# Up units of the gated networks: 64-column products in pairs instead of 128-column products

## The chip, the cores and the metric

The kernel runs on one core of a Trainium2 chip. The metric is the device time of one execution in microseconds. A core has a matrix engine (PE, which the profile splits into its matmuls, PE, and its weight loads, PEld), a vector engine (DVE), an activation engine (ACT), a general engine (POOL), and 16 DMA engines that the queues of SP, ACT and POOL feed.

## What is computed

Two stacks of two layers each, on 256 tokens of 1,024 values in float32. The first stack has two kinds of attention, a gated network of width 2,816 in its first layer (a "dense" network) and eight experts of width 3,584, of which each token takes two, in its second. Each layer of the second stack has a gated network, a mixer with three branches, and another gated network. The part that matters here is the gated network, of which there are five in all (one dense, four in the second stack):

```
def swiglu(h, w_in, w_out):
    a, b = jnp.split(h @ w_in, 2, axis=-1)      # 1024 -> 2 x 2816
    return (jax.nn.silu(a) * b) @ w_out         # 2816 -> 1024
```

## The kernel before

All weights are streamed once through a ring in the on-chip memory. The ring has four slots of 6,144 words in each partition (SLOTS, UNIT), and a slot's first 4,096 words take one 2 MB load. SP issues the loads in order (lines 434 and around), each as soon as PE has counted the slot's last use in the semaphore unit_used.

A network (the function network, line 647) has eleven up units of 256 columns of each of the two weight matrices (FFN_STEPS), and then the down products. The first up unit (whole_unit) is made as plain products of 128 columns of weights over all 1,024 rows, and in the networks of the second stack in two token halves of 128. The other ten (up_unit, line 672) are made by a scheme that needs seven block products where a plain 2 x 2 block product needs eight: DVE adds and subtracts weight blocks ahead of time (sum_weights, four additions of 128x1024 per unit, lines 1585 to 1593) and token blocks once per network (sum_tokens), PE makes seven groups of products, and ACT and DVE fold the seven results into four (line 1304, and the seven additions of fold at lines 1616 to 1625).

Each of the seven groups is done for both weight matrices (m), and adds up four products (k, over half of the 1,024 rows), so an up unit has 7 x 2 x 4 = 56 products. Each has 128 rows and 128 columns of weights, 128 columns of tokens, and a result of 128x128 in PSUM. In float32 the trace shows every matmul call as two weight loads and two matmuls, called records below, so the unit has 112 records. The calls go through the helper product (line 597), which most of the kernel uses, so the records of the up units stand at L597 beside others.

```python
for j, (lhs, rhs) in enumerate(...):            # the seven groups, line 693
    for m in range(2):
        mm = product([(up_group(q, j, m), lhs(m, k), rhs(k)) for k in range(KT // 2)])
mm.then_inc(unit_used, 1)
```

An up unit waits first for its load, for its four sums of weights, and for the fold of the unit two before it (lines 675 to 679). Units 1 to 8 are two rounds of a hardware loop whose body holds four units (Fori, line 703); units 9 and 10 are straight code (line 706). up_group puts the results of a unit in four banks of PSUM, and the next unit's in the other four. ACT and DVE work on one unit's results while PE makes the next.

The down products follow (line 718): seven products of 128x128 weights by 512 columns for each of eleven pairs of hidden blocks, by the same scheme.

The experts already use calls of 64 columns in pairs: gather (line 763), chosen_up (line 788) and chosen_down (line 798) split 128 columns of weights in GROUPS = 2 strips of STRIP = 64 that write PSUM partitions 0 to 63 and 64 to 127, one after the other for each k. The moving side there has 96 columns of tokens for the three busiest experts and 80 for the other five (TIERS). Their loop body holds seven units of 32 + 16 calls and runs four rounds per expert.

Of the kernel before, what the change touches and what calls it, by code (L numbers as in the profile page):

```python
# [19 lines left out]
KT = D // P  # L20
# [67 lines left out]
GROUPS = 2  # L88
STRIP = P // GROUPS
# [106 lines left out]
def build(nc, a, out):  # L196

    with ExitStack() as ctx:
# [182 lines left out]
        def landed(c, turns):  # L381

            return loaded[c % SLOTS], 16 * (c // SLOTS + 1) + 16 * turns

        def up_weights(c):

            return slot(c, 2 * KT, FF_STEP).rearrange("p (m k) n -> p m k n", m=2)
# [6 lines left out]
        def up_group(u, j, m):  # L394

            at = j * SEQ + m * P
            return psum[:, 4 * (1 - u % 2) + at // 512, at % 512:at % 512 + P]
# [20 lines left out]
        def banks(jobs, name):  # L418
            b = 2 * FIXED_PAIR.get(name, jobs[name] % 4)
            return psum[:, b:b + 2]  # L420
# [160 lines left out]
        def _(pe):  # L581
# [4 lines left out]
            def count_unit(m):  # L586
                if open_units[0]:
                    m.then_inc(unit_used, open_units[0])
                    open_units[0] = 0
# [4 lines left out]
            def product(terms):  # L594

                for i, (o, lhs, rhs) in enumerate(terms):
                    m = pe.matmul(o, lhs, rhs, start=i == 0, stop=i == len(terms) - 1)  # L597
                    if i == 0 and len(terms) > 1:
                        count_unit(m)
                return m  # L600
# [46 lines left out]
            def network(which, c0, turns, begin=None, finish=None):  # L647
# [24 lines left out]
                def up_unit(u, q, t):  # L672

                    w, sums = up_weights(c0 + q), weight_sum[q % 2]
                    pe.wait_ge(*landed(c0 + q, t))
                    pe.wait_ge(*ffn["weight_sum"].by(which, 4 * u))
                    if q == 2:
                        pe.wait_ge(*ffn["gated"].by(which, 2))
                    pe.wait_ge(*ffn["folded"].by(which, FOLDS_AHEAD + 7 * (u - 2)))

                    def of_weights(i, kk):
                        return lambda m, k: w[:, m, kk * KT // 2 + k, i * P:(i + 1) * P]

                    def of_sums(j):
                        return lambda m, k: sums[:, j, m, k, :]

                    def of_tokens(kk, h):
                        return lambda k: xT[:, kk * KT // 2 + k, h * P:(h + 1) * P]

                    def of_token_sums(j):  # L690
                        return lambda k: token_sum[:, j, k, :]

                    for j, (lhs, rhs) in enumerate(((of_weights(0, 0), of_tokens(0, 0)), (of_sums(1), of_token_sums(1)),
                                                    (of_weights(0, 1), of_tokens(1, 0)), (of_sums(2), of_token_sums(2)),
                                                    (of_sums(0), of_token_sums(0)), (of_sums(3), of_tokens(1, 1)),
                                                    (of_weights(1, 1), of_token_sums(3)))):
                        for m in range(2):
                            mm = product([(up_group(q, j, m), lhs(m, k), rhs(k)) for k in range(KT // 2)])
                    mm.then_inc(unit_used, 1)

                whole_unit()
# [18 lines left out]
                for p in range(FFN_STEPS - 4):  # L720
                    pe.wait_ge(*landed(c0 + FFN_STEPS + p // 2, turns))
                    pe.wait_ge(*ffn["down_sum"].by(which, 8 * p + 8))
                    for name in ("P1", "P6", "P2", "P7", "P5", "P3", "P4"):
                        if p == 0 and name == "P5":
                            pe.wait_ge(*ffn["folded"].by(which, FOLDS_AHEAD + 7 * (FFN_STEPS - 1)))
                        m = down(p, name)
# [6 lines left out]
                for p in range(last - 3, last + 1):  # L733
                    pe.wait_ge(*landed(c0 + FFN_STEPS + p // 2, turns))
                    pe.wait_ge(*ffn["down_sum"].by(which, 8 * p + 8))
                    for name in ("P1", "P6", "P5", "P2", "P3"):
                        m = down(p, name)
# [7 lines left out]
                for name in ("P7", "P4"):  # L745
                    for p in range(last - 2, last + 1):
                        if name == "P4" and p == last and finish is not None:
                            finish()
                        m = down(p, name)
# [118 lines left out]
            for l in range(LAYERS):  # L868
# [8 lines left out]
                if l == 0:  # L877
                    for i in range(KT // 2):
# [3 lines left out]
                        for h in range(HALVES):  # L882
                            for k in (2 * i, 2 * i + 1):
                                m = pe.matmul(banks(J, "latent0")[:, h, :], xT[:, k, h * P:(h + 1) * P], w[:, k, :],  # L884
                                              start=k == 0, stop=k == KT - 1, skip_group_check=True)
                else:
                    pe.wait_ge(*landed(c, 0))
                    for h in range(HALVES):
                        pe.wait_ge(*f["turned_x"].by(0, 3 + h))
                        for k in range(KT):  # L890
                            if h == 0 and k == KT - 2:
                                turn_end(1)
                            m = pe.matmul(banks(J, "latent0")[:, h, :], xT[:, k, h * P:(h + 1) * P], w[:, k, :], start=k == 0, stop=k == KT - 1)
# [9 lines left out]
                for name in ("dq0", "dq1", "dk0", "dk1", "dv0", "dv1"):  # L903
# [7 lines left out]
                    if l == 0 and name in ("dq0", "dq1", "dk0", "dk1"):  # L911
# [3 lines left out]
                        for r in (2 * i, 2 * i + 1):  # L915
                            pe.wait_ge(*once["ind"].by(0, 2 + 8 * (r + 1)))
                            for n in range(4):
                                m = pe.matmul(banks(J, f"bias{i}")[32 * n:32 * n + 32, r % 2, 0:MAP], block_delta, reached[r % 2][:, n], start=True, stop=True)
# [8 lines left out]
                for name, k_tiles, width, source in (("uq", 3, 384, cqT), ("ukv", 2, 512, ckvT)):  # L927
                    pe.wait_ge(*landed(c, 0))
                    w = slot(c, k_tiles, 2 * width)
                    for h in range(HALVES):  # L930
                        pe.wait_ge(*banks_free(f"{name}{h}", l))
                        pe.wait_ge(*f["cqT" if name == "uq" else "ckvT"].by(l))
                        for n in range(2):
                            m = row_product(banks(J, f"{name}{h}")[:, n, 0:width], w, k_tiles, width, source, h, n * width)
# [3 lines left out]
                for name, source, ready in (("q", qrow, "q_rot"), ("k", kcat, "kcat")):  # L938
                    if name == "k":
                        pe.wait_ge(*f["kv_rows"].by(l))  # L940
                    for i in range(2):
# [3 lines left out]
                        for n in range(4):  # L945
                            for h in range(HALVES):
                                m = pe.transpose(o[0:MLA_QK, n * SEQ + h * P:n * SEQ + (h + 1) * P], source[:, h, 4 * i + n, :], ident[:])
# [9 lines left out]
                for i in range(MAPS1 + 3):  # L957
# [10 lines left out]
                    if i < MAPS1:  # L968
                        pe.wait_ge(*banks_free(f"scores{i}", l))
                        for m in range(2):  # L970
                            if i < PAIRS1:
                                q, k = qT[0:MLA_QK, 2 * i + m, :], kT[0:MLA_QK, 2 * i + m, :]
                            else:
                                q, k = dqT[64 * m:64 * m + 64, i - PAIRS1, :], dkT[64 * m:64 * m + 64, i - PAIRS1, :]
                            mm = map_scores(banks(J, f"scores{i}")[:, m], q, k)
                        mm.then_inc(f["full"].sem, 1)
                    if 0 <= i - 2 < MAPS1:
# [3 lines left out]
                        for m in range(2 if h < PAIRS1 else 1):  # L981
                            mm = turn_map(banks(J, f"turn{h}")[:, m], T[:, h % 2, m])
                        mm.then_inc(f["full"].sem, 1)
                    if 0 <= i - 3 < MAPS1:
# [4 lines left out]
                        if h < PAIRS1:  # L989
                            mm = pair_values(o, PT[:, h % 2], lambda m, half: vrow[:, half, 2 * h + m, :])  # L990
                        else:
                            w, vh = PT[:, h % 2, 0], dv[:, :, (h - PAIRS1) * P:(h - PAIRS1 + 1) * P]
                            pe.matmul(o[:, 0:P], w[:, 0:P], vh[:, 0], start=True, stop=True)
                            mm = product([(o[:, P:2 * P], w[:, P:2 * P], vh[:, 0]), (o[:, P:2 * P], w[:, 2 * P:MAP], vh[:, 1])])
# [35 lines left out]
                for h in range(HALVES):  # L1030
                    pe.wait_ge(*banks_free(f"mix{h}", l))
                    m = half_rows(J, f"mix{h}", m1T, h, c, 0, f["mT"].by(l, 3), f["mT"].by(l), (lambda: turn_x(0)) if h else None)
# [35 lines left out]
                for h in range(HALVES):  # L1068
# [4 lines left out]
                    m = half_rows(J, f"ple_gate{h}", xT, h, c, 0, ready, ready, rank_tokens if l == h == 1 else None, 0)  # L1073
# [28 lines left out]
            for l in range(LAYERS):  # L1102
# [42 lines left out]
                for h in range(HALVES):  # L1145
                    half_ready(1, h)
                    for k in range(KT):
                        if h == 0 and k == 5:
                            turn_half("mix", 1, 1)
                        m = pe.matmul(banks(J, "a_v")[:, h, :], xT[:, k, h * P:(h + 1) * P], w[:, k, :], start=k == 0, stop=k == KT - 1)  # L1150
# [13 lines left out]
                for h in range(HALVES):  # L1164
                    m = row_product(banks(J, "b_kv")[:, 1, h * P:(h + 1) * P], w, KT, P, xT, h, P)
# [14 lines left out]
                for g in range(A_GROUPS):  # L1180
                    for h in range(HALVES):
                        m = pe.matmul(o[:, g * SEQ + h * P:g * SEQ + (h + 1) * P], v2[:, h, g * P:(g + 1) * P], wsT[:, g, :], start=True, stop=True)
# [6 lines left out]
                for h in range(C_HEADS):  # L1189
                    m = pe.transpose(o[:, h * P:(h + 1) * P], c_kT[:, h, 0:P], ident[:])  # L1190
# [8 lines left out]
                for i in range(MAPS2 + 3):  # L1199
# [4 lines left out]
                    if i < MAPS2:  # L1204
                        pe.wait_ge(*banks_free(f"scores{i}", l))
                        for m in range(2):
                            mm = map_scores(banks(J, f"scores{i}")[:, m], bqT[64 * m:64 * m + 64, i, :], bkT[64 * m:64 * m + 64, i // 2, :])
                        mm.then_inc(s["full"].sem, 1)
                    if 0 <= i - 2 < MAPS2:
# [3 lines left out]
                        for m in range(2):  # L1213
                            mm = turn_map(banks(J, f"turn{h}")[:, m], T[:, h % 2, m])
# [10 lines left out]
                for h in range(C_HEADS):  # L1225
                    for n in range(HALVES):
                        m = pe.matmul(o[:, h * SEQ + n * P:h * SEQ + (n + 1) * P], c_kT[:, h, n * P:(n + 1) * P], c_qT[:, h, n * P:(n + 1) * P], start=True, stop=True)
# [7 lines left out]
                for h in range(C_HEADS):  # L1235
                    m = pe.matmul(o[:, h * C_V:(h + 1) * C_V], c_kw[:, h, :], cv[:, 0, h * C_V:(h + 1) * C_V], start=True, stop=True)
                m.then_inc(s["full"].sem, 1)
                for n in range(HALVES):
# [6 lines left out]
                    for h in range(C_HEADS):  # L1245
# [3 lines left out]
                        m = product(terms)  # L1249
# [21 lines left out]
                for h in range(HALVES):  # L1271
                    pe.wait_ge(*(s["ycT"] if h else s["gate"]).by(l))
                    m = half_rows(J, f"out{h}", m2T, h, unit[0], turns, s["mT"].by(l, 5), s["mT"].by(l), (lambda: turn_half("ffn2", 2, 0)) if h else None)
# [1095 lines left out]
```

## Time and profile before

| what | us |
|---|---|
| median of three runs | 3244.98 (3243.61 to 3247.26) |
| the profiled execution | 3246.58 |
| its span, first to last instruction | 3245.0 |
| PE busy in it | 3193.5 (98%) |
| PEld busy | 2624.8 (81%) |
| DVE busy | 1049.6 (32%) |
| ACT busy | 414.4 (13%) |

The page has the busy time of every engine, the span in 40 slices with the clock that PE was granted, the DMA queues, the chain of work that ended last (followed back from the last instruction), and the costliest groups of instructions. A busy time of PE sums overlapping records, whose latency is longer than the distance between two starts. So what a product costs is read from the length of an unbroken run of records divided by their number, as the chain in order of time gives both, and not from the mean length of a record.

### The profile page before, as it was taken

The numbers are of one execution on the slowest core, as the hardware profiler recorded it, in microseconds if no ns is written. First come the engines' busy times: TensorE is split into PE (matmuls) and PEld (weight loads), VectorE is DVE, ScalarE is ACT, GpSimd is POOL, SyncE is SP. The second block draws the span as 40 slices with busy tenths as digits, with TensorE's granted clock in tenths as the row PEclk, the third lists the DMA queues.
The fourth block names the chain that finished last, engine by engine and source line by source line (L and its number), as shares of the span: only waits on it lengthen the run. The fifth ranks groups of instructions, "written<-read, shape, count | busy, mean of one in ns | idle before, by whom it ended". The sixth has DMA issues, their size and how long they took to land.

```text
span 3245.0 us, 76028 instructions
## 1 busy us (share of the span) xinstructions
PE 3193.5 (98%) x34760; PEld 2624.8 (81%) x34760; DVE 1049.6 (32%) x2232; ACT 414.4 (13%) x1031; POOL 50.6 (2%) x86
## 2 busy tenths in 40 slices
PE   9999999999999999999998999999999999999999
PEld 6685985777699999999997966588895976688894
DVE  2252564043201101111013561211566562210465
ACT  1240000042111100000001001110100001110100
POOL 0000000000000000000000000000000000000000
PEclk9999999999999999999998999999999999999999
DMA  7423444333699899999996444334444444434442
GB/s 253 151 99 152 182 160 177 139 108 120 248 388 357 355 399 376 426 426 426 426 426 271 158 172 170 130 130 156 156 158 166 175 156 169 157 108 151 156 175 91
DMA packets 63087, 714.03 MB, mean 220 GB/s; under 512 B 7569, under 2 KB 9233, under 8 KB 11889
## 3 DMA queue, kind: packets, MB, share of 16 engines
q1 hardware_dynamic: 59328, 703.62, 55.7%
q0 software_dynamic: 1008, 5.94, 0.5%
q10 hardware_dynamic: 2624, 2.65, 0.4%
q8 instruction: 96, 1.57, 0.2%
q14 instruction: 31, 0.25, 0.0%
HBM read 709.30 MB, written 1.05 MB: 219 GB/s over the span
## 4 chain that ended last, share of the span: by engine, by line
PE 94%; DMA 3%; DVE 2%; ACT 1%; POOL 1%; issue 0%; SPq 0%; POOLq 0%; DVEq 0%; ACTq 0%
PE psum L597 50%; PE psum L788 15%; PE psum L718 10%; PE psum L798 8%; PE psum L853 5%; DMA weight_ring<-in_experts 3%; PE psum L817 1%; PE psum L1150 1%; PE psum L763 1%; PE psum L635 1%; PE psum L631 1%; PE psum L884 1%; POOL statistics L519 0%; PE psum L630 0%; PE psum L1124 0%
## 5 line engine op out<-in xcount | busy, mean ns | idle before, releaser
L597 PE MATMUL psum<-arena,weight_ring 128*128 128x256 f32 (+1 forms) x5408 | 974.2, 339 | 7.9 <-DVE arena L2069 3.8
L597 PEld LDWEIGHTS psum<-arena,weight_ring 128*128 128x128 f32 x5408 | 869.4, 191 | 98.4 <-issue 14.5
L788 PE MATMUL psum<-arena,weight_ring 128*64 128x80 f32 (+1 forms) x14336 | 570.5, 238 | 6.8 <-DMA weight_ring<-in_experts 2.6
L788 PEld LDWEIGHTS psum<-arena,weight_ring 128*64 128x64 f32 x14336 | 547.9, 137 | 16.1 <-issue 8.1
L597 PE MATMUL psum<-weight_ring,arena 128*128 128x128 f32 (+3 forms) x3024 | 511.2, 326 | 2.0 <-DVE arena L1839 2.0
L597 PEld LDWEIGHTS psum<-weight_ring,arena 128*128 128x128 f32 x3024 | 385.9, 192 | 113.9 <-issue 106.8
L798 PE MATMUL psum<-arena,weight_ring 128*64 128x80 f32 (+1 forms) x7168 | 302.2, 238 | 2.4 <-issue 2.4
L1727 DVE TENSOR_TENSOR arena<-arena,psum 128x80 f32<-128x80 f32 (+1 forms) x224 | 54.7, 244 | 722.6 <-ACT arena L1317 722.6
L798 PEld LDWEIGHTS psum<-arena,weight_ring 128*64 128x64 f32 x7168 | 282.6, 137 | 2.8 <-issue 2.8
L853 PE MATMUL psum<-weight_ring,arena 128*128 128x512 f32 x384 | 168.6, 597 | 0.0
L1317 ACT ACTIVATE arena<-psum 128x80 f32<-128x80 f32 (+1 forms) x224 | 54.5, 243 | 744.8 <-PE psum L788 744.8
L853 PEld LDWEIGHTS psum<-weight_ring,arena 128*128 128x128 f32 x384 | 72.9, 192 | 87.4 <-issue 87.2
L597 PE MATMUL psum<-arena 128*128 128x128 f32 (+3 forms) x1072 | 135.7, 279 | 0.0
L718 PE MATMUL psum<-weight_ring,arena 128*128 128x512 f32 x270 | 135.4, 592 | 0.0
L597 PEld LDWEIGHTS psum<-arena 128*128 128x128 f32 (+1 forms) x1072 | 126.3, 185 | 2.1 <-issue 1.0
L718 PE MATMUL psum<-weight_ring 128*128 128x512 f32 x260 | 125.4, 592 | 0.0
L1616 DVE TENSOR_TENSOR weight_ring<-weight_ring,psum 128x256 f32<-128x256 f32 x50 | 21.1, 422 | 261.2 <-ACT weight_ring L1304 261.2
L718 PEld LDWEIGHTS psum<-weight_ring 128*128 128x128 f32 x260 | 49.4, 190 | 62.2 <-issue 62.2
L718 PEld LDWEIGHTS psum<-weight_ring,arena 128*128 128x128 f32 x270 | 50.6, 190 | 60.3 <-issue 60.3
L597 PE MATMUL psum<-weight_ring 128*128 128x128 f32 x800 | 97.5, 275 | 0.0
L597 PEld LDWEIGHTS psum<-weight_ring 128*128 128x128 f32 x800 | 93.3, 192 | 0.0
L718 PE MATMUL psum<-arena,weight_ring 128*128 128x512 f32 x180 | 86.2, 592 | 0.0
(265 smaller groups left out, 2002.7 us busy)
## 6 DMA issues: line engine op xcount, KB each, us to landing
weight_ring<-in_experts SPq DMA_DIRECT2D x224, 1536.0 KB, 11.7
weight_ring<-in_ffn_up SPq DMA_DIRECT2D x44, 2048.0 KB, 7.7
weight_ring<-in_second_wide SPq DMA_DIRECT2D x42, 2048.0 KB, 7.7
weight_ring<-in_first_wide SPq DMA_DIRECT2D x35, 2048.0 KB, 7.7
weight_ring<-in_ffn_down SPq DMA_DIRECT2D x20, 2048.0 KB, 7.7
weight_ring<-in_dense_up SPq DMA_DIRECT2D x11, 2048.0 KB, 7.9
weight_ring<-in_dense_down SPq DMA_DIRECT2D x5, 2048.0 KB, 7.6
weight_ring<-in_ffn_down SPq DMA_DIRECT2D x4, 1024.0 KB, 5.0
```

The lines of the kernel that those rows point to most:

```text
L597: m = pe.matmul(o, lhs, rhs, start=i == 0, stop=i == len(terms) - 1)
L631: return pe.matmul(o[:, P:MAP], q[:, P:SEQ], k, start=True, stop=True)
L635: m = pe.transpose(o[:, n * P:(n + 1) * P], weights[:, n * P:(n + 1) * P], ident[:])
L718: return pe.matmul(psum[:, bank], lhs, rhs, start=p == 0, stop=p == FFN_STEPS - 1, skip_group_check=True)
L763: mm = pe.matmul(psum[g * STRIP:(g + 1) * STRIP, 6 + k // 4, k % 4 * CAP:k % 4 * CAP + tokens], X[:, h, at:at + STRIP], slots_hot[:, h, 0: ...
L788: mm = pe.matmul(psum[g * STRIP:(g + 1) * STRIP, q % 4, m * CAP:m * CAP + tokens], w[:, m, k, g * STRIP:(g + 1) * STRIP], chosen[:, k, 0:t ...
L798: mm = pe.matmul(psum[g * STRIP:(g + 1) * STRIP, 4 + k // 4, k % 4 * CAP:k % 4 * CAP + tokens], w[:, at:at + STRIP], hT[:, q % 4, 0:tokens ...
L817: m = pe.matmul(psum[:, 2 + 2 * h + n], tokens_hot[0:CAP, h, :], expert_rows[0:CAP, n * 512:(n + 1) * 512], start=True, stop=True)
L853: m = pe.matmul(banks(jobs, name)[:, n, :], lhs[:, k, half * P:(half + 1) * P], w[:, k, :], start=k == 0, stop=k == KT - 1, skip_group_che ...
L884: m = pe.matmul(banks(J, "latent0")[:, h, :], xT[:, k, h * P:(h + 1) * P], w[:, k, :], start=k == 0, stop=k == KT - 1, skip_group_check=True)
L1317: nc.scalar.activation(sil[:, q % 2, 0:tokens], psum[:, q % 4, 0:tokens], ACT.Silu).then_inc(moe["silu"].sem, 1)
L1727: v.tensor_tensor(hT[:, q % 4, 0:tokens], sil[:, q % 2, 0:tokens], psum[:, q % 4, apart:apart + tokens], ALU.mult).then_inc(moe["gated"].s ...
```

## The change

In up_unit, and nowhere else, each product of 128 columns of weights becomes two calls of 64 columns. The first takes columns 0 to 63 of the same weight block and writes PSUM partitions 0 to 63 of the same place, the second takes columns 64 to 127 and writes partitions 64 to 127. The two follow each other within each k, so two sums of four terms run side by side. The operands, the order of k, the places of the results, and the semaphore at the end of the unit are as before. The helper product is no longer used there, and with it goes its count_unit on the first product of a group, which does something only if a finished unit is still uncounted; the first product of whole_unit has counted it by then. The first unit and the down products stay as they are. An up unit has 112 calls and 224 records, where it had 56 and 112.

```diff
@@ -695,7 +695,10 @@
                         for m in range(2):
-                            mm = product([(up_group(q, j, m), lhs(m, k), rhs(k)) for k in range(KT // 2)])
+                            for k in range(KT // 2):
+                                for g in range(GROUPS):
+                                    part = slice(g * STRIP, (g + 1) * STRIP)
+                                    mm = pe.matmul(up_group(q, j, m)[part], lhs(m, k)[:, part], rhs(k), start=k == 0, stop=k == KT // 2 - 1)
                     mm.then_inc(unit_used, 1)
```

## Rows read from the trace of the kernel before

**Rows 1.** The page: busy time, granted clock and instruction queues.
```profile
PE 3193.5 (98%) x34760; PEld 2624.8 (81%) x34760; DVE 1049.6 (32%) x2232; ACT 414.4 (13%) x1031; POOL 50.6 (2%) x86
...
PEclk9999999999999999999998999999999999999999
...
q8 instruction: 96, 1.57, 0.2%
```
**Rows 2.** The page: shares of the chain that ended last, by engine and by line.
```profile
PE 94%; DMA 3%; DVE 2%; ACT 1%; POOL 1%; issue 0%; SPq 0%; POOLq 0%; DVEq 0%; ACTq 0%
PE psum L597 50%; PE psum L788 15%; PE psum L718 10%; PE psum L798 8%; PE psum L853 5%; DMA weight_ring<-in_experts 3%; PE psum L817 1%; PE psum L1150 1%; PE psum L763 1%; PE psum L635 1%; PE psum L631 1%; PE psum L884 1%; POOL statistics L519 0%; PE psum L630 0%; PE psum L1124 0%
```
**Rows 3.** The chain in order of time (start, us, what): up parts of two networks.
```profile
332.41 138.88 PE psum L597 x1184
471.29 59.24 PE psum L718 x138
...
1767.77 134.00 PE psum L597 x1200
1901.77 65.23 PE psum L718 x152
```
**Rows 4.** The chain from 1774 to 1888 us: up units alone.
```profile
1773.91 114.12 PE psum L597 x1022
```
**Rows 5.** The chain: other products of 128 columns of weights, by width.
```profile
237.77 31.08 PE psum L597 x144
...
2048.67 27.47 PE psum L597 x64
```
**Rows 6.** Timeline of PE from 842 to 850 us: products 8 columns wide.
```profile
843.75 3.63 PE L597 MATMUL psum<-arena 128*128 128x8 f32 x32
```
**Rows 7.** Groups of weight loads, shapes apart (rows*columns, operand, count; busy, mean ns).
```profile
L788 PEld LDWEIGHTS psum<-arena,weight_ring 128*64 128x64 f32 x14336 | 547.9, 137 | 16.1 <-issue 8.1 <-DMA weight_ring<-in_experts 6.8 <-ACT arena L1329 1.1
L597 PEld LDWEIGHTS psum<-weight_ring 128*128 128x128 f32 x800 | 93.3, 192 | 0.0
L840 PEld LDWEIGHTS psum<-identity,x_rows 128*128 128x128 f32 x48 | 5.5, 140 | 4.6 <-DVE x_rows L1932 2.5 <-issue 2.1
L918 PEld LDWEIGHTS psum<-weight_ring,arena 128*32 128x32 f32 x64 | 1.7, 109 | 2.9 <-issue 2.9
```
**Rows 8.** The chain: transposes of 128 columns, between 292 and 298 us.
```profile
292.89 0.87 PE psum L840 x8
```
**Rows 9.** The chain in the experts: pairs, 96 columns of tokens, then 80.
```profile
1044.51 5.28 PE psum L788 x128
1051.11 2.64 PE psum L788 x64
...
1283.32 2.21 PE psum L788 x64
1285.53 1.11 PE psum L798 x32
```
**Rows 10.** The chain in the experts: full-array products between pairs.
```profile
985.29 3.63 PE psum L817 x8
```
**Rows 11.** Busy time in stretches: an up part, then three of the experts.
```profile
core 0: us, PE busy (x) PEld busy (x) DVE busy (x) ACT busy (x) POOL busy (x), PEclk, DMA share, GB/s
1767.77:1901.77 134.00, 134.00 (x1201) 134.00 (x1201) 79.93 (x134) 10.95 (x24) 0.00 (x0) 1.00 0.43 157
1040.00:1090.00 50.00, 50.00 (x1218) 50.00 (x1216) 3.30 (x13) 5.84 (x15) 0.00 (x0) 1.00 1.00 399
1280.00:1299.00 19.00, 19.00 (x557) 19.00 (x554) 1.43 (x6) 1.58 (x7) 0.00 (x0) 1.00 1.00 424
1227.20:1252.80 25.60, 22.37 (x630) 21.89 (x629) 3.66 (x10) 1.67 (x7) 0.00 (x0) 1.00 0.77 299
```
**Rows 12.** The chain in the first loop round of the fourth expert.
```profile
1245.34 1.35 issue
1246.70 0.56 PE psum L788 x9
1247.26 1.11 PE psum L798 x32
1248.36 2.21 PE psum L788 x64
1250.58 0.77 PE psum L798 x22
1251.34 1.46 issue
1252.81 1.67 PE psum L798 x41
```
**Rows 13.** Timeline of ACT and of DVE between 1774.7 and 1801 us (first of eleven, last).
```profile
1789.24 0.37 ACT L1304 COPY weight_ring<-psum 128x256 f32<-128x256 f32 x1 [12.12 <-PE psum L597]
...
1789.65 0.42 DVE L1616 TENSOR_TENSOR weight_ring<-weight_ring,psum 128x256 f32<-128x256 f32 x1 [12.07 <-ACT weight_ring L1304]
...
1795.50 1.23 DVE L1593 TENSOR_TENSOR arena<-weight_ring,arena 128x1024 f32<-128x1024 f32 x1
```

## The prediction

> **What bounds the kernel now.** I read first the page's busy times and the chain that ended last. PE is busy 98% of the span [rows 1] and makes 94% of the chain, and half of the chain stands at L597, where the up units lie [rows 2]. So time taken from PE there comes off the span, unless another engine is close behind. The granted clock is at its full level but for one slice of 40, the 22nd, at the end of the experts [rows 1], and 1.00 in the up part [rows 11]; that is the level of 2.4 GHz, so the clock has nothing to give.
>
> Then the chain in order of time. The up part of a network is one unbroken piece: 134.00 us for 1200 records in the second stack, 138.88 us for 1184 in the dense network [rows 3]. Of the 1200, 80 belong to the first unit and 10 x 112 = 1120 to the ten up units. Inside, 1022 records take 114.12 us [rows 4], so **a record costs 111.66 ns** and a product of two records 223.3 ns. Nothing else shows between them.
>
> What sets 111.66 ns? It is not the moving side. A record 512 columns wide costs 27.47 us / 64 = 429.2 ns, one 256 wide 31.08 us / 144 = 215.8 ns [rows 5]. From these a column costs (429.2 - 215.8) / 256 = 0.834 ns, and a record of 128 columns should cost 215.8 - 128 x 0.834 = 109.1 ns. On the other side, 32 records only 8 columns wide, with the same 128 columns of weights, take 3.63 us, some 110 ns each [rows 6], though their moving side would be done in 7 ns. So there is a floor at about 110 to 112 ns that does not come from tokens. Weight loads show where: a load of 32 columns lasts 109 ns, of 64 columns 137, of 128 columns 192 [rows 7], so 55 ns for each 64 columns on top of a fixed part, 110 ns for 128. Transposes, whose loads of 128 columns last only 140 ns [rows 7], go at 0.87 us / 8 = 108.8 ns with 128 moving columns [rows 8]. My reading: at 128 columns of tokens the weight load (about 111.7 ns) is just longer than the matmul (about 109.2 ns), and PE pays the longer.
>
> **The change part by part.**
>
> The pace of pairs. Two calls to different halves of the array are shown at two widths. At 96 columns 128 records take 5.28 us, 41.25 ns each; at 80 columns 64 records take 2.21 us, 34.5 ns each [rows 9]. Since two run side by side, a pair of records costs 82.5 ns and 69.1 ns. If two loads of 64 columns went one after the other, no pair could be below 2 x 55 = 110 ns; both are. So loads to the two halves overlap, and a pair costs what the tokens cost: the slope is (82.5 - 69.1) / 16 = 0.84 ns a column, the same 0.834 as for the full array. For 128 columns: 82.5 + 32 x 0.834 = 109.2 ns. The three estimates for a record without the load's floor are 108.8, 109.1 and 109.2; I take 109.2, as it comes from pairs, and 0.84 as slope would give 109.4.
>
> The gain. A network's up units had 1120 records and now have 1120 pairs of records. Each is 111.66 - 109.2 = 2.46 ns shorter: 2.76 us in a network, **13.8 us in five**. Bounds: 108.8 ns gives 16.0 us, 109.4 ns gives 12.7.
>
> Changing between full array and halves. PE now does this twice in a network (into the up units, and back for the down products). The experts do it around their eight wide products: 3.63 us for 8 records [rows 10] against 8 x 0.429 = 3.43, so 0.20 us for both changes. Five networks: **1.0 us** lost. Some of those 0.2 us may be other things, so the bounds are 0 and 1.0.
>
> Other engines. They wait for the end of a unit. ACT copies the first result of unit 1 at 1789.24, so unit 1 ended and unit 2 began just before, near 1789.0. DVE then folds from 1789.65, and has the weight sums of unit 3 done at 1795.50 + 1.23 = 1796.7 [rows 13]. Unit 3 starts one unit of 112 x 111.66 ns = 12.51 us after unit 2 did, at 1801.5, which is 4.8 us later than its sums. With units of 112 x 109.2 = 12.23 us this becomes 4.5 us. The wait for the fold two units back ends at the last addition of the fold, before these sums. DVE is busy 60% of the up part and DMA 43% [rows 11]; a gain of 2.2% in a unit doesn't bring either near. Costed at nothing; if DVE's cover were gone, each unit would wait for DVE. No wait is added, and no DMA or queue is moved. ACT and DVE read the same places of PSUM at the same event.
>
> The sum: 3245.0 - 13.8 + 1.0 = 3232.2 us of span. The profiled execution took 3246.58, 1.6 more than its span, and lies 1.6 above the median of the runs. Taking the 12.8 us off the median gives **3232.2 us**, 0.39% less. This kernel's measurement tells about 0.2%, some 6.5 us, from no change.
>
> **The rivals.**
>
> *The pace stays.* The floor of 111.7 ns could belong to something that the pairs keep, such as float32 weights read from memory at a fixed rate for both halves together. Then nothing is won and the changes cost 1.0 us: 3246. Against it, the pairs at 69.1 ns load the same 128 columns per pair, at DMA share 1.00 [rows 9, 11]. What they don't show is a busy DVE beside them (1.43 of 19 us there, 79.93 of 134 here [rows 11]). I give it 0.12.
>
> *A smaller gain.* Each side-by-side start costs some ns more at 128 columns, or beside DVE: with 1.5 ns more on each of 5600 pairs, 8.4 us of the 13.8 go, and 3240.6 is left. 0.07.
>
> *Instructions come too late; slower than before.* PE now gets twice as many instructions for its time. In the experts the trace shows what that can do: in the first round of a loop, code not run before, the chain has gaps named issue of 1.35 and 1.46 us [rows 12], in which PE waits for nothing that the profile shows, and later rounds have none (PE busy 19.00 of 19 us [rows 11]). I take it that new code isn't there yet. From the end of one gap (1246.70) to the end of the next (1252.81) PE had 6.11 us of which 4.65 us ran; that is 4.65 us / 34.5 ns = 135 records in 6.11 us, a supply of one record each 45.3 ns. The changed units want one each 109.2 / 2 = 54.6 ns. So supply is faster than demand by 9 ns, and that from a stretch with DMA share 0.77, above the 0.43 of the up part [rows 11]: no gaps. It turns if the supply in the networks is slower than 54.6 ns a record. Price: a network has six units of new code (four in the loop, two behind), 6 x 224 = 1344 records, 10 stretches of 135; with 1.4 us lost in each, as above, 14 us in a network and 70 in five: 3232 + 70 = 3302. The second round of the loop could need the same again if its body, now 4 x 224 records, isn't kept; the experts' body of 7 x 96 = 672 records is kept. 0.09 for this in any strength; a tenth of the price already takes half of the gain.
>
> **How the numbers follow.** The forecast holds 0.72, with its own range 3228.5 (108.8 ns, no cost of changing, and 0.5 us of scatter) to 3236. The pace stays: 0.12. A smaller gain: 0.07. Late instructions: 0.09, about a third of it so weak that the time is still under 3246. The range of 8 in 10 reaches from the forecast through the smaller gain to the middle of the first rival: 3228 to 3246. Faster by over 0.2% (under 3238.5): the forecast's 0.72 and a little of the smaller gain and of weak gaps, 0.75. Within 0.2%: 0.18. Slower: 0.07.
>
> **What the profile after would show.** In the chain, the up part of a network of the second stack as 80 + 2240 records in 131.3 us and not 134.0, with records 54.6 ns apart on average. Weight loads of the up units 128*64 at 137 ns. PE's matmul records 5600 more in number. More packets on the instruction queue than 96 [rows 1], and no piece named issue in the up parts; if there is one, the third rival holds. The piece of the down products stays at 65.2 and 59.2 us [rows 3]. If a record stays at 55.8 ns, the load was not what held the old products, or two loads share a rate. If the pieces of DVE or DMA appear in the chain within the up part, the cover that I read as 4.5 us was not there.

## The result, and the profile after

The changed kernel takes 3265.49 us (median of 4 runs), the kernel before 3244.83: a ratio of 1.0064, with a 95% interval of 1.0052 to 1.0076. It is slower by 20.7 us, where 12.8 us less were forecast. The profiled execution spans 3263.5 us against 3245.0.

The page of the changed kernel shows PE as busy as before, the same clock in all slices of 40, and 168 packets on the instruction queue where [rows 1] had 96:

```profile
PE 3192.6 (98%) x40360; PEld 2620.2 (80%) x40360; DVE 1049.6 (32%) x2232; ACT 413.9 (13%) x1031; POOL 50.5 (2%) x86
...
PEclk9999999999999999999998999999999999999999
...
q8 instruction: 168, 2.75, 0.3%
```

The chain in order of time (start, us, what) shows the place. This is the network whose up part was one piece in [rows 3]:

```profile
1782.91 49.08 PE psum L701 x896
1831.99 0.02 issue
1832.02 0.38 ACT weight_ring L1307
1832.40 0.02 issue
1832.42 0.42 DVE weight_ring L1619
...
1834.08 0.43 DVE weight_ring L1626
1834.51 0.11 issue
1834.62 2.61 PE psum L701 x43
1837.23 2.93 issue
1840.16 72.90 PE psum L701 x1301
1913.06 65.43 PE psum L721 x152
```

L701 is the new call. The first 896 records, units 1 to 4, go at 49.08 us / 896 = 54.8 ns, as forecast (54.6). Then comes what the prediction did not have: PE stands for 2.6 us, makes 43 records, and stands again for 2.9 us. The 896 records are one round of the loop, so the first stop lies exactly at its jump back. The chain puts ACT and DVE into the first stop, the fold of unit 4; the experiments below show that this is only what was running beside it. All five networks stop at that place. Four more pieces of the same chain, each the end of units 1 to 4 or the start of the down products, give the lengths of the up units:

```profile
345.69 49.08 PE psum L701 x896
...
477.83 59.44 PE psum L721 x138
...
2318.53 49.08 PE psum L701 x896
...
2445.69 65.43 PE psum L721 x152
```

The ten up units take 132.1 us in the dense network, 130.2 in the second, 127.2 in the third, and by the same reading 127.5 and 126.9 in the last two. Before, they took 1120 x 111.66 ns = 125.1 us each [rows 4]. The differences are 7.1, 5.1, 2.1, 2.5 and 1.9 us, 18.6 together, where the two spans differ by 18.5.

PE's clock falls behind the stops. The dense network in three stretches (busy times with counts, then PEclk, DMA share, GB/s):

```profile
394.70:402.60 7.90, 1.59 (x15) 1.15 (x13) 7.37 (x12) 1.00 (x2) 0.00 (x0) 0.64 0.75 268
402.60:407.10 4.50, 4.50 (x42) 4.50 (x44) 0.28 (x1) 0.00 (x0) 0.00 (x0) 0.50 0.01 4
407.10:477.80 70.70, 70.70 (x1296) 70.53 (x1292) 40.28 (x72) 5.01 (x10) 0.00 (x0) 1.00 0.42 151
```

In 7.9 us PE was busy for 1.6. In the next 4.5 us it had work all the time, but at 0.50 of its clock, the 1.2 GHz level, and made 42 records, 107 ns each. Then it is back at 2.4 GHz.

### The profile page after: what moved, and what is told of

The parts are those of the page before. It is cut to its first block, busy times and chain, and to the rows that moved or that the text cites. A ratio compares the mean times of both kernels' runs of the same rounds, so it can differ in the third digit from the quotient of the medians.

```text
span 3263.5 us, 87228 instructions
## 1 busy us (share of the span) xinstructions
PE 3192.6 (98%) x40360; PEld 2620.2 (80%) x40360; DVE 1049.6 (32%) x2232; ACT 413.9 (13%) x1031; POOL 50.5 (2%) x86
## 4 chain that ended last, share of the span: by engine, by line
PE 94%; DMA 2%; DVE 2%; ACT 1%; issue 1%; POOL 1%; SPq 0%; POOLq 0%; DVEq 0%; ACTq 0%
PE psum L597 30%; PE psum L701 19%; PE psum L791 15%; PE psum L721 10%; PE psum L801 8%; PE psum L856 5%; DMA weight_ring<-in_experts 2%; PE psum L820 1%; PE psum L1153 1%; PE psum L766 1%; PE psum L635 1%; PE psum L631 1%; PE psum L887 1%; POOL statistics L519 0%; PE psum L630 0%
## 5 line engine op out<-in xcount | busy, mean ns | idle before, releaser
L597 PE MATMUL psum<-arena,weight_ring 128*128 128x256 f32 (+1 forms) x3808 | 780.0, 366 | 7.7 <-DVE arena L2072 3.8
L597 PEld LDWEIGHTS psum<-arena,weight_ring 128*128 128x128 f32 x3808 | 682.9, 191 | 98.1 <-issue 14.3
L791 PEld LDWEIGHTS psum<-arena,weight_ring 128*64 128x64 f32 x14336 | 546.9, 137 | 16.4 <-issue 8.9
L701 PE MATMUL psum<-weight_ring,arena 128*64 128x128 f32 x4800 | 286.9, 274 | 3.0 <-issue 2.9
L801 PEld LDWEIGHTS psum<-arena,weight_ring 128*64 128x64 f32 x7168 | 281.4, 137 | 2.1 <-issue 2.1
L701 PEld LDWEIGHTS psum<-weight_ring,arena 128*64 128x64 f32 x4800 | 273.1, 138 | 3.5 <-issue 3.5
L597 PE MATMUL psum<-weight_ring,arena 128*128 128x512 f32 (+3 forms) x624 | 226.9, 522 | 2.0 <-DVE arena L1842 2.0
L701 PE MATMUL psum<-arena,weight_ring 128*64 128x128 f32 x3200 | 204.9, 279 | 17.1 <-DVE weight_ring L1626 10.6
L701 PEld LDWEIGHTS psum<-arena,weight_ring 128*64 128x64 f32 x3200 | 189.3, 141 | 19.8 <-DVE weight_ring L1626 11.5
L597 PEld LDWEIGHTS psum<-weight_ring,arena 128*128 128x128 f32 x624 | 109.9, 190 | 113.9 <-issue 106.8
L856 PEld LDWEIGHTS psum<-weight_ring,arena 128*128 128x128 f32 x384 | 72.9, 192 | 87.4 <-issue 87.2
L721 PEld LDWEIGHTS psum<-weight_ring,arena 128*128 128x128 f32 x270 | 50.6, 190 | 61.1 <-issue 61.1
L721 PEld LDWEIGHTS psum<-weight_ring 128*128 128x128 f32 x260 | 49.4, 190 | 62.2 <-issue 62.2
L701 PE MATMUL psum<-weight_ring 128*64 128x128 f32 x1600 | 98.5, 273 | 0.0
```

Of the source, the lines that this page charges most:

```text
L701: mm = pe.matmul(up_group(q, j, m)[part], lhs(m, k)[:, part], rhs(k), start=k == 0, stop=k == KT // 2 - 1)
L721: return pe.matmul(psum[:, bank], lhs, rhs, start=p == 0, stop=p == FFN_STEPS - 1, skip_group_check=True)
L791: mm = pe.matmul(psum[g * STRIP:(g + 1) * STRIP, q % 4, m * CAP:m * CAP + tokens], w[:, m, k, g * STRIP:(g + 1) * STRIP], chosen[:, k, 0:t ...
L801: mm = pe.matmul(psum[g * STRIP:(g + 1) * STRIP, 4 + k // 4, k % 4 * CAP:k % 4 * CAP + tokens], w[:, at:at + STRIP], hT[:, q % 4, 0:tokens ...
L856: m = pe.matmul(banks(jobs, name)[:, n, :], lhs[:, k, half * P:(half + 1) * P], w[:, k, :], start=k == 0, stop=k == KT - 1, skip_group_che ...
```

## The experiments

Three theories. A: the body of the loop has doubled, from 448 records to 896, and no longer stays in the store from which PE takes its instructions; the jump back has to wait for it. B: PE waits for DVE's fold, as the chain has it. C: instructions at this rate come too late wherever they are new, as the third rival said.

**Straight pairs.** The loop of PE is written out.

```diff
-                with pe.Fori(0, 2) as g:
+                for g in range(2):
                     for q in range(1, 1 + SLOTS):
                         up_unit(SLOTS * g + q, q, turns + g)
```

> The changed kernel, with the hardware loop over units 1 to 8 on PE written out as straight code; same products, same waits. Theory A (the jump back of the loop finds its code gone, since the body has doubled, and has to fetch it again): no stop of 2.8 to 3.2 us after unit 4, no lower clock behind it, the up part of a network of the second stack 131.6 us (8.93 + 2240 x 54.78 ns), and 3232 us in all, about 13 below before. Theory B (the chain of the changed kernel names DVE's fold of unit 4 ahead of unit 5: PE waits for DVE): the stop stays, 3265 us. Theory C (new code at this rate comes too late by itself): stops appear in all units, at least as many in units 5 to 8 as in units 1 to 4, over 3265 us.

Measured: 3234.41 us against 3245.74 before, ratio 0.9965 (0.9953 to 0.9977). The chain:

```profile
1766.21 8.93 PE psum L597 x80
1775.15 122.42 PE psum L701 x2240
```

Not one stop in 2240 records, and in no network. ACT and DVE do the same work with the same waits, so B falls. All 2240 records are new code here, so C falls too. Without the jump, pairs bring what was forecast for them: 122.42 us in place of 125.06, 2.6 us a network.

**The control**, the kernel before with the same loop written out.

> Control: the kernel before (products of 128 columns), with the same loop of PE written out. All theories: 3244.8 us within 0.1%, since its jump back costs PE nothing (the up part is one unbroken piece of 134.0 us). If this is faster by some us, the jump had a cost in the kernel before that I have not seen, and the gain of straight pairs is not that of the pairs.

Measured: 3243.44 us, ratio 0.9995 (0.9986 to 1.0004). In its chain the up part of the second network is 134.00 us, as before. So the jump back cost nothing before, and the gain of straight pairs is one of pairs (9.0 us by the medians against this control, whose own 2.3 us under the kernel before aren't clear of noise). Its instruction queue shows what straight code costs in fetching. Against [rows 1] it runs 5 x 448 records more as new code:

```profile
q8 instruction: 114, 1.87, 0.2%
```

This is 18 packets of 16.4 KB more for 2240 records, so one packet holds some 124 records, with the loads and matmuls counted apart some 250 instructions. A body of 896 records is 7.2 packets, one of 448 is 3.6.

**How large a body is kept.** The loop stays, and units 3 and 4 of its body, or unit 4 alone, keep products of 128 columns.

```diff
                         for m in range(2):
+                            if q == 4:          # e3: if q in (3, 4)
+                                mm = product([(up_group(q, j, m), lhs(m, k), rhs(k)) for k in range(KT // 2)])
+                                continue
```

> As the last, with the third and fourth unit of the body in products of 128 columns: 2 x 224 + 2 x 112 = 672 matmul records in the body, as many as the experts' body has, which the trace shows to loop without a stop. Theory A: no stop, 6 of 10 units gain, 8.2 us, less up to 2 us for changes of form: 3238 to 3239. Theory B: the stop gets shorter by 0.3 us at most, about 3266. Theory C: fewer stops in proportion.

Measured with 672 records in the body: 3240.13 us, ratio 0.9986 (0.9976 to 0.9995). No stop in any network. An up part is 133.2 us, 0.8 us less than before, where six of ten units in pairs would have brought 1.6; the rest goes to four more changes of form in it, whose price comes below.

> The changed kernel with the loop kept, but the fourth unit of the body (units 4 and 8) in products of 128 columns: the body has 3 x 224 + 112 = 784 matmul records in place of 896. Theory A: either this body is kept, then 8 of 10 units gain (11 us), two more pairs of changes of form in a network cost up to 2 us, 3235 us; or it isn't, then the stop after unit 4 remains: 22 us of stops and up to 10 of a lower clock on top, about 3265. Theory B: PE is slower in unit 4, so DVE has more time: the stop gets shorter by 0.3 us.

Measured with 784 records: 3249.21 us, ratio 1.0011 (1.0002 to 1.0021), between the two outcomes I had written down. The chain shows why. First the dense network, then another:

```profile
344.98 36.83 PE psum L704 x672
381.81 12.72 PE psum L597 x112
...
396.23 0.86 PE psum L704 x11
397.09 4.64 issue
401.73 38.32 PE psum L704 x661
```
```profile
1783.36 36.83 PE psum L704 x672
1820.19 12.70 PE psum L597 x112
1832.89 36.83 PE psum L704 x672
1869.72 12.70 PE psum L597 x112
1882.42 24.60 PE psum L704 x447
```

The same body stops in the dense network, where its up part takes 146.2 us, and loops without a stop in the other four (132.6 us each). The instruction queue agrees; packets in the up part of the dense network, then of the second network:

```profile
q8 instruction: 19, 0.31, 0.8%
```
```profile
q8 instruction: 10, 0.16, 0.5%
```

**The same body, moved.** By 124 records a packet this body is 6.3 packets. If code comes in blocks that lie at fixed places, it can lie across seven of them or across eight. The next kernel is the last one with the dense network's first unit made in calls of 64 columns, which takes the same time (13.96 us for 13.81), but puts 64 records, 128 instructions, more ahead of the loop.

```diff
...
+                                if begin is not None:
+                                    mm = product([(place, w[:, m, k, i * P:(i + 1) * P], xT[:, k, tokens]) for k in range(KT)])
+                                    continue
+                                for k in range(KT):
+                                    for g in range(GROUPS):
+                                        part = slice(g * STRIP, (g + 1) * STRIP)
+                                        mm = pe.matmul(place[part], w[:, m, k, i * P:(i + 1) * P][:, part], xT[:, k, tokens], start=k == 0, stop=k == KT - 1)
...
```

> Three of four units in pairs, loop kept, where the dense network alone had stopped for 2.0 and 4.9 us after unit 4 and the other four networks had not, with the same body of 784 records. Here the first unit of the dense network has its 32 products (256 columns of tokens, so pairs bring nothing there) in calls of 64 columns: the work takes the same time, but all code behind it lies 128 instructions further on. Theory D (whether a body is kept depends on how it lies on the blocks of 256 instructions in which code is fetched: seven blocks are kept, eight are not): the dense network's stop goes, its up part falls from 146.3 to about 137.2 us, and the whole to 3240; at another network a stop of the same kind may appear instead, as its code moves too. Theory E (the dense network differs by its data or its loads): the stop stays in it, 3249 us.

Measured: 3237.56 us, ratio 0.9971 (0.9960 to 0.9982), 12 us less by the medians than the kernel it was made from. The dense network, whose first unit is now at L671:

```profile
332.37 13.96 PE psum L671 x128
346.33 36.68 PE psum L712 x672
383.01 12.70 PE psum L597 x112
395.71 36.83 PE psum L712 x672
432.55 12.70 PE psum L597 x112
445.25 24.60 PE psum L712 x448
```

The stop is gone (137.5 us), and none appeared elsewhere. The up part of this network shows 11 instruction packets, where it had 19. So where the code lies decides, and not the data or the loads of this network. The chain accounts for 8.7 of the 12 us; no run tells where the others come from, and the two profiled executions differ by 6.6 us only.

**The size without pairs.** The full array, but two calls with 64 columns of tokens each, so the body again has 896 records. (The sums of this kernel come out wrong; it is read for its times only.)

```diff
-                            mm = product([(up_group(q, j, m), lhs(m, k), rhs(k)) for k in range(KT // 2)])
+                            for k in range(KT // 2):
+                                for t in range(2):
+                                    part = slice(t * P // 2, (t + 1) * P // 2)
+                                    mm = pe.matmul(up_group(q, j, m)[:, part], lhs(m, k), rhs(k)[:, part], start=k == 0, stop=k == KT // 2 - 1, skip_group_check=True)
```

> The kernel before with its loop, each product of 128 columns of weights made as two calls with the same 128 columns and 64 token columns each. The body has 4 x 224 = 896 records, as in the changed kernel, but no call for half the array. Weight loads bound each record at 111.7 ns or less, so an up part takes 8.9 + 2240 x 111.7 ns = 259 us and the whole 3870. Theory A (size of the body): PE stops after unit 4 in every network, by less than 3.3 us since its queue now holds twice the time: 1 to 3 us. If it is the pairs that make the jump slow: no stop.

Measured: 4574 us in one run. The stop after 896 records is there in all five networks. The second:

```profile
2042.75 100.01 PE psum L701 x896
2142.76 0.02 issue
2142.78 0.38 ACT weight_ring L1307
...
2144.28 0.20 issue
2144.49 286.45 PE psum L701 x1344
```

It lasts 1.7 us, shorter than with pairs (2.6 us), as expected; that PE still has more work in its queue when the jump begins to wait is my reading, and no run shows it. The size of the body is enough to bring the stop, without any pairs. And with half the tokens in a call a record of the first 896 takes 111.6 ns, as with 128: what sets that floor isn't the tokens. The time of the whole is 700 us more than I expected, and the last row has it: 286.45 / 1344 = 213 ns a record, 136 us more than at 111.6 ns, and so in each of the five networks. The last section comes back to it.

**What a change of form costs.** Straight code, pairs in every second of the seven groups.

```diff
+                            if j % 2 == 0:
+                                mm = product([(up_group(q, j, m), lhs(m, k), rhs(k)) for k in range(KT // 2)])
+                                continue
```

> Straight code, groups 1, 3 and 5 of the seven in pairs and groups 0, 2, 4 and 6 in products of 128 columns: six changes of form in an up unit, 300 in all, where straight pairs have 10. With 0.098 us a change as read from the experts' wide products, 29 us are lost and 3/7 of 13 us won: 3268 us. If a change costs nothing, 3239.

Measured: 3292.36 us, ratio 1.0142 (1.0124 to 1.0161).

```profile
1789.77 1.90 PE psum L704 x32
1791.66 1.98 PE psum L597 x16
1793.64 1.90 PE psum L704 x32
1795.54 1.98 PE psum L597 x16
```

16 records in full form should take 1.79 us and take 1.98; 32 in pairs should take 1.75 and take 1.90. That is 0.35 us for two changes, 0.17 us for one and not 0.098. 300 changes come to 52 us, and 3/7 of the 13.2 us of the straight kernel is 5.7, so 46 us more than before, as measured. In the straight kernel there are only two changes in a network.

**The order of the calls.** Straight code, all four calls for one half ahead of the four for the other.

```diff
-                            for k in range(KT // 2):
-                                for g in range(GROUPS):
+                            for g in range(GROUPS):
+                                for k in range(KT // 2):
```

> Straight code, the same calls of 64 columns, but in a sum the four calls of the first half of the array come first, and then the four of the second, where the pairs take turns. If the two halves run side by side only where the next instruction is for the other half (as I read the experts), most calls now wait for the one before: 7 of 8 records of a sum follow one of their own half, 109.2 ns each, and the up units take nearly 2240 x 109.2 = 245 us per network in place of 122.5; about 3234 + 5 x 115 = 3800 us. If PE reaches far enough ahead to run the halves side by side in any order, 3234 us.

Measured: 3311 us in one run. The chain from 1790 to 1900 us:

```profile
1789.95 110.07 PE psum L701 x1785
```

61.7 ns a record, against 54.7 where the halves take turns and 109 had they run one after the other. So turns are worth 7 ns a record, but the halves overlap for the most part even without them. The starts of single records show how. Those that read weight_ring alone belong to the last sum of a unit, those with arena to the first sum of the next:

```profile
1799.83 0.32 PE L701 MATMUL psum<-arena,weight_ring 128*64 128x128 f32 x1
1799.93 0.27 PE L701 MATMUL psum<-weight_ring 128*64 128x128 f32 x1
1799.99 0.27 PE L701 MATMUL psum<-arena,weight_ring 128*64 128x128 f32 x1
```

The first half of the next sum runs beside the second half of this one. My reading of the pairs was too narrow.

**Pairs for the first unit as well.** The 32 products of the first unit in the four networks of the second stack (80 + 48 records with 128 columns of tokens) also go in pairs; the edit is that of the moved kernel, for the other networks.

> The straight code with pairs, and the first unit of the four networks of the second stack (32 products of 128 token columns in each half, 128 records in all) in pairs as well. If the gain is one of pace, 512 records of 111.7 ns become 512 pairs of 109.4: 1.2 us less than with straight pairs alone, so 3233 us and nothing lost in new changes of form. If the pace of pairs leans on something in the up units alone, no difference.

Measured: 3246.60 us, ratio 1.0002 (0.9993 to 1.0011). The four networks gained, 131.15 us where straight pairs take 131.35, but by a slip in the edit the dense network made its first unit twice, which took 151.1 us and hid the rest. Without the slip:

> As e4, but without its slip: e4 made the first unit of the dense network twice, once in products of 128 columns and once in pairs, so that this network's up part took 151.2 us and not 136.3. Here it is made once, in products of 128 columns, and only the first units of the four networks of the second stack are in pairs. From the parts of e4 and e1: four up parts of 131.15 us and one of 136.3, which is 1.2 us less than straight pairs alone: 3232 to 3233 us, 0.37 to 0.4% below before.

Measured: 3232.23 us against 3245.89, ratio 0.9958 (0.9944 to 0.9971). Its chain:

```profile
1763.53 8.88 PE psum L671 x160
1772.41 122.27 PE psum L709 x2240
```

It has the lowest median of all the kernels, and beats both the kernel before and the changed one. Against straight pairs alone the chain shows 0.2 us a network; the whole times don't separate the two (0.9958 and 0.9965, with intervals that overlap).

## Why the prediction was wrong

*What bounds the kernel* was right: what PE lost at this place is the whole of the difference, to 0.1 us.

*The pace of pairs* was right, and its reason is borne out. The forecast was 109.2 ns a pair; the changed kernel shows 109.6 in its first four units, straight code 109.3. That the tokens don't set the old 111.7 ns is shown by the kernel with halved tokens, which keeps it. The gain of 13.8 us less 1.0 comes out as 5 x (134.0 - 131.35) = 13.2 us in the chain of the straight kernel (8.93 + 122.42 against 134.00), and as 11.3 us by the medians. DVE at 58% of the up part, which the experts' pairs did not have beside them, doesn't slow pairs.

Two rows were read loosely, without effect on the forecast. The 32 narrow records of [rows 6] come to 3.63 / 32 = 113 ns, the latency of the last one included, so "some 110" is a guess at what is left without it. And the stretch between the gaps of [rows 12] shows 127 records, not 135, so a supply of one each 48 ns, not 45.3, still ahead of the demand.

*Changes of form* were under-sized, 0.17 us for 0.098. With two in a network this is at most 0.7 us in the sum. The 4 ns for a further tile of the Trainium skill (TensorE: Matmul & The Clock Gate, "Measured speedup vs the span model"), by which 110.7 ns were to be expected, an estimate from the page, are not borne out: 109.3.

*Other engines* was right in what it looked at, ACT, DVE, DMA and the waits, and **failed in what it left out**: it took the loop as it was. A loop is a wait too if its body isn't there any more. I treated instructions as a stream with a rate, supply of 45.3 ns against demand of 54.6, and on that the third rival was judged. That comparison held: straight code is all new, and has no stop. So my sign, that a piece named issue would mean the third rival, would have misled. The step that failed is the sentence on the second round, "could need the same again if its body, now 4 x 224 records, isn't kept; the experts' body of 7 x 96 = 672 records is kept". There lay the case, with both numbers beside each other, and I used the 672 as comfort without asking whether 896 is on the same side. I then priced it as more of the same stream, not as a jump to code that has to be fetched first. The runs put the limit between: 672 is kept, 784 is kept or not by where it lies, 896 is not kept in any of the five. The instruction queue of the changed kernel shows the fetch itself. In each network a packet starts 0.1 to 0.2 us before the end of the 896 records, and PE goes on 2.7 to 3.1 us after that. In the second network this is the one packet between 1831.8 and 1831.9.

The Trainium skill (Runtime: NRT & Kernel Launch, "Instruction fetch mechanics") has this as a rule that I had not weighed. It says that PE's instruction store holds 2048 instructions, is refilled in blocks of 16 KiB, 256 instructions, and that a taken branch to code that is not in the held window waits for a DMA. The 16.4 KB a packet agree, and so does the stop at the jump. The 2048 do so in part: 784 records, some 1570 instructions, can be kept, but 896, some 1800, aren't, though they are fewer than 2048. That only two blocks are held, as the same section has it, does not agree, since bodies of 448 to 784 records, 3.5 to 6 blocks by the page's size (an estimate), loop here with no stop.

*The price.* The stops and what follows them cost 132.1 - 122.4 = 9.7 us in the dense network, and 7.7, 4.7, 5.1 and 4.5 us in the others: 31.8 us together, against the 13 us won. In the second network 5.6 us of the 7.7 are stops, and the rest is for the most part PE at a lower clock after them. The second stop goes with the next packet. It starts 5.4 to 6.4 us after the first in all five networks, in the second between 1837.8 and 1837.9. Where PE stands again, it goes on 2.2 to 2.4 us after this packet's start. What differs is how many records it made in between: 11, 43, 63 and 70 in the first four networks, with second stops of 3.39, 2.93, 0.06 and 0.24 us (the packet of the fourth came latest); the fifth has none. This fits loops that start at different distances from the end of a block: few records left, long stop. The dense network makes 11 records between its two stops in the changed kernel, in the one with 784 records and in the one with halved tokens, and the code ahead of its loop is the same in all three. If that loop starts 11 records before the end of a block, its body of 784 lies across eight blocks (773 / 124 = 6.2 more). Moved by 64 records, it has 71 in its first block and lies across seven (713 / 124 = 5.8 more), and there its stop was gone. No run moved the second stop by itself, so this is a reading of the traces. The exact number of blocks that are kept stays open: the runs say that 6.3 packets' worth can be kept and 7.2 packets' worth isn't.

*The chances.* 0.09 for late instructions in any strength was too little for a resource that the change doubled and for which no row of before bounded 896.

## What to carry to other kernels

If an edit multiplies the instructions in a hardware loop, count the instructions of the body against the largest body that the trace shows to loop without a gap, and treat anything above as a stop at each jump back; near the limit even the position of the code decides, so leave a block of margin or write the loop out. When the chain shows another engine in a gap of PE, look whether the gap lies at a loop's jump before believing it. Where a record costs more than its tokens need (here 111.7 ns against 109.2, with 128 columns of each), look whether the weight load sets the pace; calls for the two halves of the array in turns took that away here.

## What had not been expected of the hardware

PE's clock can stay down while PE has work without a break. In the kernel with halved tokens, busy times in the second network before the stop and after it (PEclk is the third number from the end):

```profile
2042.80:2142.70 99.90, 99.90 (x896) 99.81 (x894) 23.34 (x37) 3.38 (x7) 0.00 (x0) 1.00 0.23 85
2144.50:2430.90 286.40, 286.40 (x1345) 286.40 (x1346) 46.58 (x81) 5.64 (x11) 0.00 (x0) 0.50 0.12 44
```

Records of 128 columns of weights and 64 of tokens ran at 2.4 GHz for 100 us, and after a stop of 1.7 us at 1.2 GHz for 286 us, 213 ns each, till other products followed. The other four networks of this run show the same. With pairs of 128 columns of tokens the clock was back 4.5 us after a longer stop. In this run the stream of narrow products kept the clock it came with; it did not bring it back.

PE doesn't keep strictly to the order of its calls: with four calls for one half ahead of four for the other, records of the next sum start before the last ones of this sum (the rows above), and a record costs 61.7 ns, where one after the other would make it near 109. This is one run.
